# Depthwise convolution with four interleaved time phases on the partitions: 288 dense matmuls in place of 992 diagonal ones

## The reference, cut to what matters

```
u = xn @ w_pw1 + b_pw1                 # (2048, 1024) @ (1024, 2048)
a, g = split(u, 2);  u = a * sigmoid(g)
u[t] = sum over k of w_dw[k] * u[t-30+k] + b_dw   # 31 taps, causal, each channel alone
u = silu(layer_norm(u, ln_g, ln_b))    # over the 1024 channels
h = h + u @ w_pw2 + b_pw2
```

## Time and profile before

| | us |
|---|---|
| median of 3 runs (lowest, highest) | 2767.01 (2758.22, 2770.92) |
| the profiled execution: its time / span of its slowest core | 2769.39 / 2768.3 |
| spans of the 8 cores | 2730.0 to 2768.3 |
| TensorE busy over the span | 1979.0 (71%) |
| VectorE / ScalarE / GpSimd busy | 796.5 / 959.5 / 444.7 |
| `phase_A` on the slowest core | from 0 to 556 |
| first matmul of layer 0's experts | 789 |

### The profile page before, as it was taken

How to read it: one execution, slowest core, us unless ns; L and a number is a source line. 1 busy time by engine, 2 the same in 40 slices (tenths; PEclk the granted TensorE clock), 3 DMA queues, 4 the chain that set the end, 5 groups by cost and what they waited for, 6 DMA issues and landing times.

```text
span 2768.3 us, 37361 instructions; the slowest of 8 cores (2730.0 to 2768.3 us)
## 1 busy us (share of the span) xinstructions
PE 1979.0 (71%) x11760; PEld 1077.1 (39%) x11760; DVE 796.5 (29%) x1623; ACT 959.5 (35%) x1834; POOL 444.7 (16%) x597
## 2 busy tenths in 40 slices
PE   3999992941369995557678777777794369995456
PEld 1344430310135553223345545545541235553223
DVE  2321103431433331434411111111134433331433
ACT  2311015211122221334576666676612122221323
POOL 0010004110210012144011111111101210012143
PEclk9999995875689997577799999999997679997577
DMA  9899999996159997321386666886651159997433
GB/s 242 173 128 153 138 142 141 121 158 131 62 178 322 328 314 193 125 86 44 47 103 72 82 78 81 102 98 72 123 94 69 61 172 309 325 317 209 131 124 120
DMA packets 125951, 413.01 MB, mean 149 GB/s; under 512 B 34864, under 2 KB 34864, under 8 KB 101168
## 3 DMA queue, kind: packets, MB, share of 16 engines
q0 software_dynamic: 64352, 188.76, 44.9%
q1 hardware_dynamic: 60816, 220.65, 24.6%
q10 hardware_dynamic: 576, 1.05, 0.2%
HBM read 427.99 MB, written 205.78 MB: 229 GB/s over the span
## 4 chain that ended last, share of the span: by engine, by line
PE 57%; issue 15%; ACT 9%; DMA 9%; DVE 7%; POOL 2%; DVEq 0%; ACTq 0%; POOLq 0%; SPq 0%
PE ps L256 53%; PE ps L260 5%; ACT sq L273 3%; DMA gb<-ysd,slots 3%; DMA xt<-xsd 3%; ACT pt L273 2%; DMA h<-xT 2%; DMA ring<-w 1%; DVE gb L294 1%; POOL pt L276 1%; POOL h L276 1%; ACT rt L273 1%; ACT rtD L273 1%; DVE ao L276 1%; DVE tc L276 1%
## 5 line engine op out<-in xcount | busy, mean ns | idle before, releaser
L256 PE MATMUL ps<-xTT,ring 128*128 128x384 bf16 (+1 forms) x2304 | 354.7, 315 | 2.5 <-DVE xTT L300 2.0
L256 PE MATMUL ps<-sq,ones_bf 128*128 128x512 bf16 x288 | 136.7, 489 | 286.0 <-ACT sq L273 273.2
L256 PEld LDWEIGHTS ps<-xTT,ring 128*128 128x128 bf16 x2304 | 215.3, 98 | 140.7 <-issue 5.3
L256 PE MATMUL ps<-glu,dg 128*128 128x512 bf16 x992 | 216.5, 381 | 6.2 <-DVE dg L276 6.2
L273 ACT ACTIVATE pt<-ps,cst_s 128x256 bf16<-128x256 f32 x576 | 209.5, 488 | 0.0
L260 PE MATMUL ps<-cst_s,gb 128*128 128x128 f32 x256 | 62.1, 424 | 198.7 <-DVE gb L294 155.0
L256 PEld LDWEIGHTS ps<-sq,ones_bf 128*128 128x128 bf16 x288 | 28.8, 100 | 446.8 <-issue 446.8
L256 PE MATMUL ps<-pt,vh 128*128 128x256 bf16 x576 | 148.2, 266 | 61.9 <-POOL pt L276 39.0
L273 ACT ACTIVATE sq<-h 128x512 bf16<-128x512 f32 x192 | 113.2, 623 | 216.0 <-PE ps L256 149.1
L256 PE MATMUL ps<-ring,hdn 128*128 128x512 bf16 x800 | 179.3, 379 | 0.4 <-DVE hdn L276 0.2
L256 PE MATMUL ps<-xgA,w 128*128 128x512 bf16 x768 | 175.1, 392 | 3.3 <-DVE h L294 3.3
(11 more groups left out here) (181 smaller groups left out, 2797.6 us busy)
## 6 DMA issues: line engine op xcount, KB each, us to landing
w<-w_moe POOLq DMA_DIRECT2D x96, 1024.0 KB
ring<-w SPq DMA_DIRECT2D x96, 1024.0 KB
ysd<-ysb SPq DMA_DIRECT2D x96, 512.0 KB
xt<-xsd SPq DMA_DIRECT2D x32, 768.0 KB
xsd<-zt SPq DMA_DIRECT2D x16, 1024.0 KB
ysd<-zt SPq DMA_DIRECT2D x9, 1024.0 KB
yT<-h SPq DMA_DIRECT2D x32, 256.0 KB
h<-xT SPq DMA_DIRECT2D x28, 256.0 KB
```

The source lines that it names most:

```text
L256: return self.op('pe', lambda e: e.matmul(out, lhsT=lhsT, rhs=rhs, start=start, stop=stop, **kw), ins=[lhsT, rhs], outs=[out], inc=inc)
```

## The change

The convolution gets a layout in which the 128 partitions are 32 channels times 4 time phases: partition 32*i + ch of group `g` (32 groups of 32 channels) holds position 4*u + i of channel 32*g + ch, at column u. 31 taps then reach over 9 columns, and one matmul with a 128x128 matrix (4x4 phases of diagonal 32x32 blocks) does for all 512 columns what four taps did: 9 matmuls for each group, 288 in all, each 128x512.

What comes with it:

- pw1 runs block by block (`c` outside, `tt` inside), its weights come in 8 chunks of 2 DMAs with 512-byte source rows into four buffers, and all four norms stand in its first block. VectorE writes the result with positions split by phase (`gp`).
- 16 DMAs on SP's queue for each `c` (128 in all, 32 partitions x 1 KB each) regroup `gp` into `gc`. The same number, of the same size, take the normed result from `gc` back to the channel layout for pw2.
- The convolution of block c-1 stands behind pw1 of block c. Channel sums of the norm are taken per group behind each group's convolution (64 matmuls), into two PSUM banks that stay.
- The layer norm is done once for all positions, in 32 groups; its subtraction alternates between GpSimd (19) and VectorE (13).
- pw2 reads positions in phase order, and `h` is updated with a stride of 4.
- The casts: `pump(1)` and `zero(1)` stand in pw1 of the blocks 1 to 7, one each for every (c, tt), so 28 casts there, none in the convolution, and the 20 left behind pw2. The zeros are issued on POOL's queue. `w2` is loaded on POOL's queue behind the last convolution.

```diff
-                glu = sb("glu", [128, NC8, HALO + S_LEN], BF16, pc)
+                gc = sb("gc", [128, NG, GW], BF16, pc)
+                w1 = sb("w1", [128, 4, 2, NC8, 128], BF16, p2)
+                gp = sb("gp", [128, 2, 4, TT], BF16, p2)
+                dg = sb("dg", [128, 2, 36, 4, 32], BF16, p2)
+                def load_w1(c):
+                    for q in range(2):
+                        S.dma('pool', w1[:, c % 4, q], w1v[:, :, q * D + c * 128:q * D + (c + 1) * 128])
+                load_w1(0)
+                S.dma('act', cva[:], cva_d)
+                for c in range(1, 4):
+                    load_w1(c)
...
-                        S.wait_tok('sp', (S.sem['pe'], S.cnt['pe'], 'pe'))
-                        S.dma('sp', ap[j * 128:(j + k) * 128, :].rearrange("(a p) d -> p a d", p=128),
+                        S.wait_tok('pool', (S.sem['pe'], S.cnt['pe'], 'pe'))
+                        S.dma('pool', ap[j * 128:(j + k) * 128, :].rearrange("(a p) d -> p a d", p=128),
...
-                            zero(1)
-                            if tt >= 1 and c % 2:
-                                pump(1)
...
+                def pw1(c):
+                    for tt in range(NTT):
+                        if c == 0:
+                            rms_tile(tt, 'g_mix', 0, lambda k, t1=tt: xn(k, t1 * TT, TT))
...
+                        S.act(sg[:, tt % 2, :], pg[:], AF.Sigmoid, bias=P('b_pw1', 8 + c))
+                        S.stt(gp[:, c % 2, :, tt * 128:(tt + 1) * 128].rearrange("p i u -> p u i"),
+                              pa[:].rearrange("p (u i) -> p u i", i=4), P('b_pw1', c),
+                              sg[:, tt % 2, :].rearrange("p (u i) -> p u i", i=4), ALU.add, ALU.mult)
+                        if c > 0:
+                            pump(1)
+                            zero(1)
+                    for gg in range(4):
+                        for i in range(4):
+                            S.dma('sp', gc[32 * i:32 * i + 32, 4 * c + gg, 8:GW],
+                                  gp[32 * gg:32 * gg + 32, c % 2, i, :])
+                    if c + 4 < NC8:
+                        load_w1(c + 4)
+                def conv(c):
+                    for gg in range(4):
+                        g = 4 * c + gg
+                        ps = next_ps()
+                        for v in range(9):
+                            S.mm(ps[:], dg[:, c % 2, gg * 9 + v].rearrange("p j c -> p (j c)"), gc[:, g, v:v + TT],
+                                 v == 0, v == 8)
+                        S.act(gc[:, g, 8:GW], ps[:], AF.Identity, bias=P('b_dwP', g))
+                        S.act(sq[:, g % 2, :], gc[:, g, 8:GW], AF.Square)
+                        if g:
+                            stats(g - 1)
+                for c in range(NC8 + 1):
+                    if c < NC8:
+                        build(c)
+                        pw1(c)
+                    if c:
+                        conv(c - 1)
+                stats(NG - 1)
+                p2.close()
                 w2 = sb("w2", [128, NC8, D], BF16, pc)
                 w2v = w_pw2.rearrange("(c p) n -> p c n", p=128)
                 for c in range(NC8):
                     S.dma('pool', w2[:, c, :], w2v[:, c, :])
-                        for j in range(31):
-                            S.mm(ps[:], dg[:, c % 2, j, :], glu[:, c, tt * TT + j:tt * TT + j + TT], j == 0, j == 30)
-                        S.act(cvb(c, tt), ps[:], AF.Identity, bias=P('b_dw', c))
-                        if len(casts) > 3 * NE:
-                            pump(1)
-                            zero(1)
...
+                for g in range(NG):
+                    v = gc[:, g, 8:GW]
+                    S.tt('dve' if g % 5 in (1, 3) else 'pool', t1[:, g % 3, :], v, mean[:], ALU.subtract)
+                    S.tt('dve', t2[:, g % 3, :], t1[:, g % 3, :], rstd[:], ALU.mult)
+                    S.act(v, t2[:, g % 3, :], AF.Silu, bias=P('ln_bP', g), scale=P('ln_gP', g))
+                    c, gg = g // 4, g % 4
+                    for i in range(4):
+                        S.dma('sp', xn(c, i * TT, TT)[32 * gg:32 * gg + 32, :], gc[32 * i:32 * i + 32, g, 8:GW])
...
                 while len(casts) > 3 * NE:
                     pump(1)
                 zero(len(zj))
```

More of the change, by code:

```diff
@@ L334, in prm_layout @@
     n = 0
-    for name, w in [('g_mix', 16), ('g_ffn', 16), ('g_ple', 16), ('b_pw1', 16), ('w_dw', 248), ('b_dw', 8),
-                    ('ln_g', 8), ('ln_b', 8), ('b_pw2', 8), ('q_gain', 1), ('k_gain', 1),
+    for name, w in [('g_mix', 16), ('g_ffn', 16), ('g_ple', 16), ('b_pw1', 16), ('b_dwP', 32),
+                    ('ln_gP', 32), ('ln_bP', 32), ('b_pw2', 8), ('q_gain', 1), ('k_gain', 1),
                     ('wr0', 160), ('wr1', 160), ('rb0', 20), ('rb1', 20)]:
@@ L347, in pack_params @@
     pk.add('b_pw1', feat_cols(inp['conv_b_pw1'][0]))
[L348 to L352, removed]
+    for nm, key in (('b_dwP', 'conv_b_dw'), ('ln_gP', 'conv_ln_g'), ('ln_bP', 'conv_ln_b')):
+        pk.add(nm, np.tile(np.asarray(inp[key][0], dtype=np.float32).reshape(32, 32).T, (4, 1)))
     pk.add('b_pw2', feat_cols(inp['conv_b_pw2'][0]))
@@ L368, in pack_params, with pack_conv @@
     return arr
+def pack_conv(inp):
+    wdw = np.asarray(inp['conv_w_dw'][0], dtype=np.float32).reshape(31, 32, 32)
+    wsh = np.zeros((4, 32, 32, 9, 4), dtype=np.float32)
+    for i in range(4):
+        for v in range(9):
+            for j in range(4):
+                k = 4 * v + i - j - 2
+                if 0 <= k <= 30:
+                    wsh[i, :, :, v, j] = wdw[k].T
+    p = np.arange(128)
+    blk = (p[:, None] // 32 == p[None, :] // 32).astype(np.float32)
+    m32 = (p[:, None] % 32 == p[None, :] % 32).astype(np.float32)
+    return np.ascontiguousarray(np.concatenate([wsh.reshape(128, 32 * 36), blk, m32], axis=1))
 def cst_layout():
@@ L431, in build_program @@
     cst_d = din("cst", [128, NCST])
+    cva_d = din("cva", [128, 32 * 36 + 256])
     w_pw1 = din("w_pw1", [D, 2 * D])
@@ L544, in phase_A @@
         def phase_A():
+            NG = 32
+            GW = 8 + TT
             with ExitStack() as pc:
                 xg[0] = sb('xgA', [128, NC8, S_LEN], BF16, pc)
-                rms_tile(0, 'g_mix', 0, lambda c: xn(c, 0, TT))
-                glu = sb("glu", [128, NC8, HALO + S_LEN], BF16, pc)
-                S.memset('pool', glu[:, :, 0:HALO], 0.0)
+                gc = sb("gc", [128, NG, GW], BF16, pc)
+                cva = sb("cva", [128, NG * 36 + 256], F32, pc)
+                blk = sb("blk", [128, 128], BF16, pc)
                 zt = sb("zt", [128, D], F32, pc)
+                p2 = ExitStack()
+                w1 = sb("w1", [128, 4, 2, NC8, 128], BF16, p2)
+                gp = sb("gp", [128, 2, 4, TT], BF16, p2)
+                sg = sb("sgA", [128, 2, TT], F32, p2)
+                dg = sb("dg", [128, 2, 36, 4, 32], BF16, p2)
+                w1v = w_pw1.rearrange("(c p) n -> p c n", p=128)
+                def load_w1(c):
[5 more added lines that the diff above has]
+                    load_w1(c)
+                S.memset('pool', gc[:, :, 0:8], 0.0)
                 S.memset('dve', zt[:], 0.0)
+                S.copy('dve', blk[:], cva[:, NG * 36:NG * 36 + 128])
+                m32 = cva[:, NG * 36 + 128:NG * 36 + 256].rearrange("p (j c) -> p j c", c=32)
                 zt16 = zt[:].bitcast(BF16)[:, 0:D]
@@ L586, in phase_A, with build @@
-                dg = sb("dg", [128, 2, 31, 128], BF16, pc)
+                def build(c):
+                    S.tt('dve', dg[:, c % 2], m32.unsqueeze(1).to_broadcast([128, 36, 4, 32]),
+                         cva[:, c * 144:(c + 1) * 144].rearrange("p (a j) -> p a j", j=4).unsqueeze(3).to_broadcast([128, 36, 4, 32]),
+                         ALU.mult)
+                P1, P2 = PS[6], PS[7]
+                ps_set[0] = list(range(6))
+                done = [0]
+                def pw1(c):
+                    for tt in range(NTT):
+                        if c == 0:
+                            rms_tile(tt, 'g_mix', 0, lambda k, t1=tt: xn(k, t1 * TT, TT))
+                        pa = next_ps()
+                        pg = next_ps()
+                        for k in range(NC8):
+                            S.mm(pa[:], w1[:, c % 4, 0, k, :], xn(k, tt * TT, TT), k == 0, k == NC8 - 1)
+                        for k in range(NC8):
+                            S.mm(pg[:], w1[:, c % 4, 1, k, :], xn(k, tt * TT, TT), k == 0, k == NC8 - 1)
+                        S.act(sg[:, tt % 2, :], pg[:], AF.Sigmoid, bias=P('b_pw1', 8 + c))
[4 more added lines that the diff above has]
+                            pump(1)
+                            zero(1)
+                    for gg in range(4):
[4 more added lines that the diff above has]
+                        load_w1(c + 4)
@@ new lines, in stats @@
+                def stats(g):
+                    S.mm(P1[:], blk[:], gc[:, g, 8:GW], g == 0, g == NG - 1)
```

(23 more changed lines are left out.)

33 lines of the change are left out of this document (5 added, 28 removed).

## The result

The changed kernel takes 2928.27 us (2922.98 to 3023.34, four runs), the kernel before 2768.97 on the same chip (2758.22 to 2861.7, four runs): ratio 1.0583 [1.0532, 1.0633], slower by 5.8%. Forecast were 2912 us and a range of 2845 to 2985. The profiled execution took 2932.63 us, 163 more than before's 2769.4. Its slowest core is core 3, and the rows of the changed kernel are of that one; rows of the other runs are of their slowest core, unless another is named.

What follows compares the result with a forecast made beforehand. One full software DMA queue bounds the kernel from 98.28 to about 656 us. 99 + 422 to pw2, 59 in it and 218 of casts give 798 instead of 656: +142, so 2912 us; range 2845 to 2985.

Steps and rivals of the forecast that it cites:

- When the queue starts: Block 0 of pw1: four norms in series, 20 us a tile, c=0 over and first cast at 99 us.
- From there to pw2: POOL's queue up to `w2`: casts, zeros, chunks, `w2` and regrouping take 422 us, so pw2 starts at 521.
- rival 3: SP's DMAs alternate with POOL's DMA by DMA, not packet by packet: pw2 at about 590, 2981 us; 10 in 100.
- They end about with `w2`: Packets back to the channel layout, before pw2: they end about with `w2`, near 521, adding nothing to the sum.
- +15: Range term: the way back to the channel layout ending as a tail before pw2 adds 15 us.
- Behind pw2: pw2 takes 59 us with the queue idle, then 20 casts take 218 us, the last at 798.
- near 180: ScalarE's copy into `xrow` in the router, at about 807, comes after a wait near 180 us.
- the 154 us of TensorE: Convolution: 288 matmuls at 0.218 us in place of 992 save 154 us, all hidden behind the full queue.

Runs made afterwards that it cites:

- cheap casts: Layer 0's 48 casts replaced by zero fills in both kernels, in the changed one all issued before the last convolution: 2661.25 us against 2717.8 us.
- the best order: Casts redistributed over phase A, pw2, router and expert loop: changed kernel 0.9973, then 0.990 (2750.8 us); kernel before 0.9895 (2745 us).

## Why the prediction was right

The forecast of 2912 was 16 us under the median, the sign and the mechanism held, and no rival took its place. That it came so near is in part luck: steps that were wrong by 20 to 33 us went in opposite directions. Its steps on core 3:

**When the queue starts, mis-sized by about 30 us.** "c=0 ends at 99 us" and the first cast with it; it was 132.66. The four tiles of block 0 took 20.4 us each, forecast were 20. What was wrong is where they begin: VectorE's first scaling came at 57.34, where the sum has it at about 27. ScalarE held its first work to 43.00, with the issue of `cva` in front of it in its own queue; VectorE sat 41.43 us for `cva` and builds `blk` and `dg` before the first scaling. The diff showed that load on ScalarE's queue, and I counted its bytes but not who stands behind it. With `cva` early ScalarE's first work began at 16.28, the scaling at 28.77 and the first cast 31 us sooner, which shows the cause.

**From there to pw2.** "422 us": the last packet of `w2` ended at 527, the first chunk was issued at 125.4, so 402. The queues in 125 to 528:

```profile
q0 software_dynamic: 20656, 61.08, 91.5%
q1 hardware_dynamic: 9891, 6.77, 6.7%
```

6.7% of 403 us are 27 us for the regrouping up to `w2`, where 37 stood for both ways; both ways together cost 8192 x 0.057 / 16 = 29. The larger part is the casts. By size, the trace's packets of q0 took, in us on 16 engines: casts 245 (forecast 265), zeros 83 (73), chunks 27 (29), `w2` 13 (18). An 8 KB packet took 1.09 us here on average and 1.20 at 760 to 780, where casts are alone: the price read from casts alone was too high for this stretch. Why is open; beside the zeros of the kernel before, at 140 to 160, it was 1.19. The alternation that rival 3 denied is there, 596 to 591. The Trainium skill ("DMA: Bandwidth & Descriptors", section "Queues, rings and completion order") lets an engine finish a packet of typically 9 to 17 descriptors before it turns to the other queue; the trace does not agree where the contiguous run is the descriptor, and rival 3's 2981 with it did not come.

**"They end about with `w2`", wrong by 33 us.** The 128 DMAs back were issued from 429.97 to 558.7 and pw2's long run began at 560.16. I had "+15" for such a tail in the range, none in the sum. GpSimd got free at 424 instead of 400, by its 24 semaphores, and SP needs 0.507 us for one of these DMAs, where the row I took said 0.36: 128 of them cannot be done in less than 65 us, and took 129.

**Behind pw2, as forecast.** pw2 57 us for 59; queue idle in it, share 0.04; 20 casts in one run at 617.44; the last ended at 834.6, so 217 us for 218. The copy waited 169.19 for "near 180" and came 1.7 us behind the last cast, where the forecast had 9; and then all is the same work: `xt` 114 us behind the copy in both kernels.

Sum of the deviations up to the last cast, with the queue's start taken at its first chunk, 125.4 for 99: +26 - 20 + 33 - 2 - 1 = +36; measured were 834.6, forecast 798, so +37. At the copy, 836.26 for 807, it is +29. At `xt` the kernel is 171 us behind the one before; the whole execution is 163 behind, so some 8 us come back further on. A part is the same wait as above, behind the last expert: 1.78 us in the changed kernel, 4.48 in the one before. The rest is open.

**Where the 154 us of TensorE went.** The forecast hid them entirely. With cheap casts 56 us of them show, with real ones in the best order none. The steps between: the 288 matmuls were busy for 86.3 us, 0.300 each, not the 0.218 of the forecast, so 130 us are saved and not 154; the gating writes take VectorE 2.49 us instead of 0.75; four norms in series at the start; the way back in place of the layer norm's rounds. The group of these matmuls, and one stretch of them on TensorE's timeline:

```profile
L256 PE MATMUL ps<-gc,dg 128*128 128x512 bf16 x288 | 86.3, 456 | 67.4 <-DMA gc<-gp 66.2 <-ACT gc L273 1.2
```

```profile
212.49 4.00 PE L256 MATMUL ps<-gc,dg 128*128 128x512 bf16 x9 [5.57 <-DMA gc<-gp]
...
217.13 2.37 PE L256 MATMUL ps<-gc,dg 128*128 128x512 bf16 x9
```

They come in runs of nine behind a transfer, and the first nine after a wait take 4.00 us where the next take 2.37; the stretch's granted clock is 0.85, before it was 0.99. That the some 56 us of chunk and regrouping packets, new in the queue (27 + 29), are what keeps the dense version from winning in the best order is argued from the prices, not shown.

## What to carry to other kernels

Before making an engine faster, ask which queue is full in its stage: here 704 matmuls fewer bought nothing in any order of casts that was tried, and moving 16 of 20 background transfers within a first-in, first-out queue gave back 72 to 91 us. A background transfer has a price at every place, the place where it seems free included: behind the router's last scatters it stretched the next load from 9 to 36 us, in the expert stage it cost, by the match of the numbers, its whole 9.4 us. Many small transfers on one issuing queue are priced by their issue, and a load issued from a compute engine's queue holds that engine's work behind it.

## What was not expected of the hardware

- An SP issue of a DMA over 32 partitions within SBUF took 0.507 us, against 0.36 for the zero fills.
- A 1 KB packet from SBUF to SBUF took 0.057 us with its share of 4-byte packets, as much as the 0.056 that the prediction read for 256 bytes of a weight load.
- The 4-byte packets, 16 to a DMA, take their turns too: 596 to 591 counts them.
- VectorE wrote 128x512 bf16 with its phases split apart in 2.49 us; in the kernel before the same gating took 0.75 us:

```profile
L294 DVE SCALAR_TENSOR_TENSOR gp<-ps,prm_s,sgA x32: 2476/2493/2650, 69.0 to 355.2; 128x512 bf16<-128x512 f32 x32
```
